# Two transformer blocks on one core: joined column sets and seven orders of work around TensorE

## What is computed

```python
def first_block(...):
    hx = modulate(rmsnorm(x, norm1_g), mx[:, :, 0], mx[:, :, 1])
    ux = hx @ w_in                       # queries, gates, fnet part
    ox, _, _ = hgrn_bidir(*hgrn_inputs(ux, lb), sc_f, sc_b)
    yx = merge_branches(ux, hgrn_readout(ux, ox, ...), w_a, w_b, w_out)
    x = x + mx[:, :, 2] * yx
    h2 = modulate(rmsnorm(x, norm2_g), mx[:, :, 3], mx[:, :, 4])
    x = x + mx[:, :, 5] * conv_ffn(h2, ffn_up, ..., ffn_down)
    return rmsnorm(x, final_g)

def second_block(x, mem, ...):
    x = x + hybrid_mixer(rms_norm(x, norm_mix_w), w_in, ..., w_out)   # pool and gated attention
    x = x + memory_cross_attention(rms_norm(x, ..), rms_norm(mem, ..), wq, wkv, wo)
    x = x + conv_ffn_2(rms_norm(x, norm_ffn_w), w_up, ..., w_down)
    return rms_norm(x, norm_final_w)
```

## Time and profile before

| What | Value |
|---|---|
| Median of 3 runs | 893.72 us |
| The profiled execution, own time | 894.42 us |
| Its span, first to last instruction | 892.6 us |
| Mean granted TensorE clock | 0.985 of full |
| TensorE busy | 858.7 us, 96% |
| VectorE, ScalarE, GpSimd busy | 583.2, 462.7, 441.5 us |
| DMA | 160.95 MB, mean 180 GB/s |

### The profile page before, as it was taken

One profiled execution on the slowest core, in us unless ns is written; L12 is line 12 of the kernel. 1 busy time (PEld: TensorE's weight loads), 2 busy tenths in 40 slices (PEclk: granted clock), 3 DMA queues, 4 the chain that ended last, 5 costly groups with the idle time before them and its releaser, 6 DMA issues.

```text
span 892.6 us, 16215 instructions
## 1 busy us (share of the span) xinstructions
PE 858.7 (96%) x6572; PEld 818.5 (92%) x6572; DVE 583.2 (65%) x1182; ACT 462.7 (52%) x753; POOL 441.5 (49%) x217
## 2 busy tenths in 40 slices
PE   6799999999999999999999899899999999999996
PEld 2388999998899999999999899899999999999996
DVE  6988987866767796776765769676458433433335
ACT  5332344542656665555554664455445555545555
POOL 0766412222652798888888100000003688787882
PEclk9899999999999999999999999899999999999998
DMA  9957574655375466565565446154535475655651
GB/s 344 350 210 247 181 236 163 225 166 185 134 239 187 145 191 192 182 189 184 176 187 182 134 127 204 53 167 133 174 98 163 123 211 181 187 177 186 189 166 48
DMA packets 45758, 160.95 MB, mean 180 GB/s; under 512 B 5218, under 2 KB 5490, under 8 KB 45556
## 3 DMA queue, kind: packets, MB, share of 16 engines
q1 hardware_dynamic: 45680, 159.91, 55.6%
q10 hardware_dynamic: 4, 0.01, 0.0%
HBM read 158.85 MB, written 1.05 MB: 179 GB/s over the span
## 4 chain that ended last, share of the span: by engine, by line
PE 78%; DVE 11%; ACT 4%; issue 3%; DMA 2%; POOL 1%; SPq 0%; DVEq 0%; ACTq 0%; POOLq 0%
PE bank L629 16%; PE bank L625 16%; PE bank L627 16%; PE bank L952 4%; PE bank L950 4%; PE bank L948 4%; DVE wlo L492 3%; ACT whi L1164 2%; PE bank L753 2%; PE bank L837 2%; DMA ada_kT<-in_adaT 1%; PE bank L705 1%; PE bank L694 1%; PE bank L690 1%; PE bank L692 1%
## 5 line engine op out<-in xcount | busy, mean ns | idle before, releaser
L492 POOL TENSOR_TENSOR wlo<-raw,whi 128x1024 fp32r<-128x1024 f32 (+1 forms) x177 | 411.9, 2348 | 392.2 <-ACT whi L1164 392.1
L1164 ACT ACTIVATE whi<-raw 128x1024 fp32r<-128x1024 f32 (+1 forms) x253 | 258.3, 1026 | 78.6 <-PE bank L629 41.7
L629 PE MATMUL bank<-h2l,whi 128*128 128x256 f32 x848 | 240.9, 284 | 2.4 <-DVE h2l L1572 2.4
L625 PE MATMUL bank<-h2h,whi 128*128 128x256 f32 x848 | 242.2, 286 | 0.5 <-ACT h2h L1388 0.5
L627 PE MATMUL bank<-h2h,wlo 128*128 128x256 f32 x848 | 240.4, 284 | 0.0
L1572 DVE SCALAR_TENSOR_TENSOR accs<-bank,vec,accs 128x189 f32<-128x189 f32 (+4 forms) x440 | 161.1, 432 | 72.3 <-ACT accs L1434 72.3
L629 PEld LDWEIGHTS bank<-h2l,whi 128*128 128x128 f32 x848 | 163.2, 192 | 3.5 <-DVE h2l L1572 3.5
L625 PEld LDWEIGHTS bank<-h2h,whi 128*128 128x128 f32 x848 | 163.3, 193 | 1.4 <-ACT h2h L1388 0.7
L627 PEld LDWEIGHTS bank<-h2h,wlo 128*128 128x128 f32 x848 | 163.3, 193 | 0.1
L492 DVE TENSOR_TENSOR wlo<-raw,whi 128x1024 fp32r<-128x1024 f32 x76 | 92.5, 1226 | 26.8 <-ACT whi L1164 26.3
L952 PE MATMUL bank<-gl,whi 128*128 128x256 f32 x336 | 95.2, 283 | 1.3 <-DVE gl L1569 1.3
(11 more groups left out here) (328 smaller groups left out, 1689.0 us busy)
## 6 DMA issues: line engine op xcount, KB each, us to landing
raw<-in_up SPq DMA_DIRECT2D x88, 512.0 KB, 3.6
raw<-in_w_in SPq DMA_DIRECT2D x45, 512.0 KB, 3.7
raw<-in_down SPq DMA_DIRECT2D x44, 512.0 KB, 3.6
ada_kT<-in_adaT SPq DMA_DIRECT2D x22, 512.0 KB, 4.0
raw<-in_w_out SPq DMA_DIRECT2D x16, 512.0 KB, 4.3
raw<-in_w_in_t SPq DMA_DIRECT2D x12, 512.0 KB, 4.6
ada_vM<-in_adaT SPq DMA_DIRECT2D x10, 512.0 KB, 4.3
ada_buf<-in_adaT SPq DMA_DIRECT2D x8, 512.0 KB, 10.5
```

The source lines that it names most:

```text
L492: return e.tensor_tensor(wlo[:, j % HL, 0:k], raw[:, j % RAW, 0:k], whi[:, j % HL, 0:k].bitcast(F32), ALU.subtract)
L625: e.matmul(ps, wh[:, k, :], xh(k), start=k == 0, stop=False)
L629: t = e.matmul(ps, wh[:, k, :], xl(k), start=False, stop=k == KTILES[name] - 1)
L1164: e.activation(whi[:, j % HL, 0:(k1 - k0) * 128], raw[:, j % RAW, 0:(k1 - k0) * 128], ACT.Copy).then_inc(S.hi.up(j))
```

## The change

Ten edits in the engines' hand-written programs and in the two tables; no computation is added or left out.

1. **States among columns.** `BESIDE[0]` (an fnet set) moves from behind the diagonal to between the key transposes and the states.
2. **Far blocks among columns.** They move from behind the last level's three fillers to behind the first of them.
3. **w_out 0**: its low half moves from GpSimd to VectorE, put ahead of the last product with `w_b`.
4. **First pair joined.** The columns up 0 and up 22 run by turns, in one bank (`lins(..., True)`).
5. **End of feed-forward 1.** wk 4 stands ahead of slab 20; slabs 20 and 21 are joined; wk 5 behind them; wv 0 goes away from here.
6. **Columns of w_in2.** The set of three is undone: 16, 4, 5, 6 singly, then 7, the means, 0 (with the spread), 1, and only then `gate_low`, then 2 and 3. The low half of 16 goes to GpSimd. `residual("down")` makes x new and `h2l` two tiles at a time; the high and low halves have new places among the squares.
7. **Joined means a column later.** Spread rs1 comes first, then wk 6, then the means g0 and g1, wk 7 with the spreads g0 and g1, and then wv 0. VectorE takes the two reciprocals behind the eight products of x (`second_x`).
8. **Residuals w_out2 and wo**: ScalarE makes the high half of column j + 4 ahead of `h2h` of tile j, VectorE x new ahead of the low half. w_out2 0's low half goes to GpSimd.
9. **wo in two parts.** Columns 0 and 1 are cut at k-tile 6, and `mix(3)` stands behind the first part of column 0.
10. **up2 0, 22 and 1**: their low halves move from GpSimd to VectorE.

```diff
@@ ffn of chunk_list
-            elif i == NFF + DLAG - 1:
+            elif i == NFF + DLAG - 2:
                 for name, n in beside:
...
-    ffn("up", "down", [("wk", 4), ("wk", 5)])
-    two("wv", 0)
+    ffn("up", "down", [("wk", 4)])
+    one("wk", 5)
...
     for j in (6, 7):
         one("wk", j)
+    two("wv", 0)
@@ low_by
+        if name == "up2" and n in (0, 1, NFF):
+            out.append("dve")
...
+        elif (name, n) == ("w_in2", 16):
+            out.append("pool")
...
-        elif name in ("w_a", "w_b") or (name == "w_out" and n == 0):
+        elif name in ("w_a", "w_b") or (name == "w_out2" and n == 0):
@@ lins
-                        e.matmul(ps, wh[:, k, :], xh(k), start=k == 0, stop=False)
+                        first = k == 0 and (c == cs[0] or not one_bank)
+                        e.matmul(ps, wh[:, k, :], xh(k), start=first, stop=False, skip_group_check=one_bank)
@@ pe
+            for kind, n in BESIDE[0]:
+                filler(kind, n)
             w.wait_ge(S.V, (1, 1))
...
-            for kind, n in BESIDE[0]:
-                filler(kind, n)
...
-                for kind, n in BESIDE[v + 1]:
+                for i, (kind, n) in enumerate(BESIDE[v + 1]):
+                    if v == 6 and i == 1:
+                        halves()
                     filler(kind, n)
@@ up_pair
+                if f == 0 and i == 0:
+                    lins([(up, i, banks[slot][:, 0:L], free), (up, i + NFF, banks[slot][:, L:2 * L], (None, None))], x, True)
+                    return
@@ pe, behind the first feed-forward part
-            for k in range(NFF - DLAG, NFF - 1):
-                slab(0, "down", k)
+            slab(0, "down", NFF - 3)
             mem_key(4)
+            slabs(0, "down", (NFF - 2, NFF - 1))
             mem_key(5)
-            slab(0, "down", NFF - 1)
-            mem_value(0)
...
-            lins(columns, hm)
...
+                lin("w_in2", n, banks[first + slot][:, 0:L], hm, free)
+            slot, free = lin_ring.take(("w_in2", 7), S.raw2, 7)
+            lin("w_in2", 7, banks[slot][:, 0:L], hm, free)
             means("down", M["ssum"][:, 0, :], 4, S.sums, ("down", 7), (S.by_row, "rsd"))
...
-            for n in range(4):
+            for n in (2, 3):
@@ pe, behind the heads of the second block
-            mem_key(6, lambda: [spread(f"g{n}", aux_bank(f"g{n}")) for n in range(2)])
-            mem_key(7)
+            mem_key(6)
+            for n in range(2):
+                means(f"g{n}", sq_at(("heads", 1, n)), 4, S.sqo, f"g{n}", (S.yb, (1, 2 * n + 1)), 1)
+            mem_key(7, lambda: [spread(f"g{n}", aux_bank(f"g{n}")) for n in range(2)])
+            mem_value(0)
...
-            mix(3)
-            residual("wo", of("oh", "ol", S.oh, lambda k: k // 2, S.ol, lambda k: k // 2))
+            residual("wo", of("oh", "ol", S.oh, lambda k: k // 2, S.ol, lambda k: k // 2), 2, 6, lambda: mix(3))
@@ act, residual
+                        if j < 7:
+                            splits(ch(name, j) + HL + 1)
+                        else:
+                            sqrt_next()
...
-                        if j == 3:
-                            splits(ch("wv", 0) + HL)
+                        if j == 5:
+                            splits(ch("w_in2", 4) + 1)
+                        if j == 7:
+                            splits(ch("w_in2", 5) + 1)
...
+                        if j == 1:
+                            mem_key(5)
+                        if j in (2, 5):
+                            splits(ch("w_in2", 6 + j // 5) + 1)
@@ dve
+                if j == 7:
+                    los(ch("w_out", 0) + 1)
...
-                        if j > 1:
+                        if j > 1 and j % 2:
+                            low(j - 3)
                             low(j - 2)
...
-                if h % 2:
-                    inverse(f"g{h // 2}")
             second_x()
+            for n in range(2):
+                inverse(f"g{n}")
```

More of the change, by code:

```diff
@@ L650, in lins, with lin_parts @@
                         wh, wl = weights(c)
-                        t = e.matmul(ps, wh[:, k, :], xl(k), start=False, stop=k == KT - 1)
+                        t = e.matmul(ps, wh[:, k, :], xl(k), start=False, stop=k == KT - 1, skip_group_check=one_bank)
                         if k == KT - 1:
                             t.then_inc(S.chunk.up(c))
-            def lin_parts(columns, x, cut):
+            def lin_parts(columns, x, cut, between=None):
                 xh, xl, high, high_event, low, low_event = x
@@ L672, in lin_parts @@
                             t.then_inc(S.chunk.up(c))
+                        elif between and name == columns[0][0] and n == columns[0][1]:
+                            between()
             def lin_tok(name, n, outs, x, frees):
@@ L825, in by_blocks, with halves @@
                 return bass.AP(x.tensor, x.offset, [list(x.ap[0]), [2 * c, 64 // c], [4 * L + c, 2], [1, c]])
+            def halves():
+                w.wait_ge(S.upd, 6)
+                for s in range(2):
+                    slot, free = aux_ring.take(f"far{s}", S.pick, f"far{s}")
+                    w.wait_ge(*free)
+                    for h in range(4):
+                        t = e.matmul(banks[4 + slot][:, h * 128:h * 128 + 128], kx[:, s, h, s * 128:s * 128 + 128],
+                                     Q2[:, 1 - s, h, (1 - s) * 128:(1 - s) * 128 + 128], start=True, stop=True)
+                    t.then_inc(S.score.up(f"far{s}"))
             for v in range(7):
@@ L897, in pe, with residual @@
                 lin("w_b", j, banks[slot][:, 0:L], yb, free)
-            def residual(name, x, turns=0):
+            def residual(name, x, turns=0, cut=KT - 1, between=None):
                 columns = []
@@ L905, in residual @@
                 if turns:
-                    lin_parts(columns, x, KT - 1)
+                    lin_parts(columns, x, cut, between)
                 for j in range(turns, 8):
@@ L1060, in pe @@
                 t.then_inc(S.heads.up((1, n)))
-            for n in range(2):
-                means(f"g{n}", sq_at(("heads", 1, n)), 4, S.sqo, f"g{n}", (S.yb, (1, 2 * n + 1)), 1)
             slot, free = aux_ring.take("rs1", S.x2, 0)
@@ L1441, in ffn @@
                         cut(f, i - 1)
-                for k in range(NFF - DLAG, NFF - 1):
-                    splits(ch(down, k) + HL)
+                splits(ch(down, NFF - 3) + HL)
                 silu(f, NFF - 1)
@@ L2202, in pool @@
                 mem_low(k)
-            los(ch("w_out", 0) + 1)
+            los(ch("w_b", 7) + 1)
             for k in (0, 1, 2):
```

67 lines of the change are left out of this document (26 added, 41 removed).

## The result

The changed kernel took 884.98 us (median of 8 runs, 883.39 to 889.08), the kernel before 893.84 us (median of 8, 890.38 to 895.43). The ratio is 0.991, with a 95% interval of 0.9889 to 0.9931. The forecast was 884.5 us. The profiled execution took 885.71 us, with a span of 883.8 us against 892.6.

The account below looks back on a forecast made before the run. TensorE bounds the kernel, busy 858.7 of 892.6 us, so only waits, late matmuls and low clocks can give time. Terms for these, from -5.4 to +1.65, sum to -9.9 us from 894.42: 884.5 us, range 878 to 890.

Parts of the forecast that it names:

- The wait, +0.5: First pair by turns: TensorE stands still 2.0 us for up 22's GpSimd low half, where 1.5 was lost before.
- The low clock, +1.65: First pair: one low-clock stretch added behind the new 2.0 us wait, because the 1.71 wait had one; +1.65 us.
- 1.6, 0.9 and 4.0: End of feed-forward 1: new waits for low halves before w_in2 columns 7, 1 and 3, in us.
- The 1.2 before V2: V2's low half comes 4.06 us after column 3's, with one column of 2.88 as cover: a 1.2 us wait.
- Now wk 6 covers the table load and the squares: Means g0 and g1: a column ahead hides ScalarE's table load and squares; 2.6 lost and 3.3 of low clock go.
- On VectorE the low half takes 1.22: -1.9: up2 0: its 1.71 wait for `h2l` goes once the low half moves from GpSimd to VectorE; -1.9 us.
- the -1.6 behind it: up2 0: the low clock of 3.2 us goes with the wait ahead of it; -1.6 us.
- The 1.1 of edit 9: mix(3): its 0.98 wait for PT goes, with the first parts of a column ahead; -1.1 us.
- more low clocks: Rival: the means and column 3's wait bring two more low-clock stretches of 1.65 us; 887.8 us, chance 0.20.
- a covered chain: Rival: the chain behind gate_low is covered, so waits of 4.0 and 1.2 us go; 879.3 us, chance 0.14.
- GpSimd's rule as a loss of 4.1 us: Rival: moving low halves from GpSimd to VectorE wins nothing, so 0.6 + 1.9 + 1.6 are lost; 888.6 us, chance 0.10.
- a slower kernel: Rival: the clock stays low from the wait before column 3 until the means, ending above 897 us; chance 0.03.

Follow-up runs that it names:

- pair_low_dve: Changed kernel with the low half of up 22 moved from GpSimd to VectorE, the first pair still joined: 883.30 us, ratio 0.9883 to the kernel before.
- both means_early: Changed kernel with means g0 and g1 first again, wv 0 kept behind wk 7: 887.75 us; with wv 0's first low half also on VectorE: 889.75 us.
- pair_apart: Changed kernel with the first pair's two columns run one behind the other again: 884.04 us, ratio 0.9898 to the kernel before.

## Why the prediction was right, and where it was not

- **Edits 1 to 4**: -1.27, +0.25, -0.72 and +1.90 against -1.3, +0.1, -0.6 and +2.15. For the first pair the forecast had two terms. The wait, +0.5, held: +0.44 in the five traces with a full clock. The low clock, +1.65, priced by the nearest row (1.71 idle, with a low clock), came in three of eight traces with the same wait of 1.64 or 1.65, and cost 1.5 there. That it stands in the changed kernel's trace is luck; the row that it was priced by was one execution too.
- **Edits 5 and 6**: +0.31 against +0.45. The waits were 1.34, 0.75 and 3.94 idle, 1.5, 0.9 and 4.1 with the 0.16, for a forecast of 1.6, 0.9 and 4.0. The 1.2 before V2 did not come: column 3 ran at 1.2 GHz and took 4.5 us for its 2.9, which covered it. That is the same time in another place.
- **Edit 7**: -5.74 against -5.9, the size right and its cause half wrong. The weak step is "Now wk 6 covers the table load and the squares". It had little left to cover: without that cover the means wait 0.69 with a full clock, and the new order adds 0.97. What took the wait was a low half that left VectorE's path because the table of chunks was reordered. Whether the cover would have done it alone was not run. The order's difference showed wv 0 moving; I had costed it as 5.8 us of TensorE's work and not followed its low half into the place four chunks ahead.
- **w_out2**: -0.72 against -0.2. The wait of 0.60 came as forecast; what was missed is lateness that no bracket shows: the stretch lost the 0.76 of the new wait and still got 0.72 shorter, so 1.5 was won where the last column's 0.51 had stood for 0.7. The ring was there before: 3.08 to 3.09 us from one `h2h` to the next where TensorE takes 2.88, seven times, 1.4 in all, and 2.88 in the changed kernel. Undoing edit 8 for w_out2 alone was not tried.
- **Edits 8 to 10**: -4.75 against -4.6, again with the wrong edit. "On VectorE the low half takes 1.22: -1.9" and the -1.6 behind it were put down to edit 10; the runs give them to edit 8 (6.3 us more without it), and 0.5 to edit 10. "VectorE's sums stand still beside GpSimd's low half" was read rightly; that this is what makes up2 0 wait was the wrong step. The 1.1 of edit 9 was not tried alone; the wait for PT is gone. The rule that I weighed (the Trainium skill, page "Perfetto Trace Analysis", section "Optimizing Scalar/DVE Operations": moving work between the two might not help) was borne out for this edit, and not for the first pair, where the move gave 1.0 us without a low clock on either side: there TensorE waited for that very low half.
- **Rivals**: more low clocks, a covered chain, GpSimd's rule as a loss of 4.1 us and a slower kernel did not come. The median came out 0.5 us above the forecast, which flatters it: two of the terms had the right size for a reason that was not the one given, a third (1.65) comes in some executions only, and in the trace the start's 1.5 happened to fall against a gain of 0.8 more than forecast.

## What to carry to other kernels

When a table of chunks is reordered, follow each chunk's helper work to the place where an engine does it, not only the chunk's own product: 3.3 us here came from a 1.2 us low half that left a chain by way of the table. Look for rings between two engines, in which each does work for the next step behind the answer to this one; their period, compared with the pace of the engine that is to be fed, tells what they cost, though no wait is shown until the end. And a wait behind a chain through ScalarE was taken away here by doing ahead of the chain what had queued behind it; it has to be done for all that follow, or the wait is only handed on (3.94 became 2.72 before V2, and 0 when all that queued was moved). Before a low clock is put down to an edit, look whether other traces of the same code have it.

## What was not expected of the hardware

One wait had more than one price. At the first pair eight traces show the same wait of 1.64 or 1.65 us idle: in three a stretch of 3.3 to 3.4 us at 0.50 followed, in five the clock stayed at 1.00, 26.5 us against 25.0 for the same work. Before column 3 it was 3.94 idle in all nine traces that have this wait, and a low stretch came every time, but of two lengths: 3.4 us in four (the changed kernel, pair_low_dve, both means_early), with 12.55 to 12.60 us from `gate_low` to V2, and 6.8 us in five (pair_apart among them), with 13.41 to 13.43. There it began some 1.5 us before column 3 started, while TensorE still stood idle. None of the waits of 1.33 to 1.37 us idle before w_in2 7, in eleven traces, had a low clock behind it. So the price of a wait can't be read from one execution; here it differed by 1.5 us in one place and 0.8 in the other.

The unchanged start of the program differed by up to 2.8 us between executions and the stretch from the heads to w_out by up to 4.4, more than most of the edits are worth.
